# Expert-list selection by 256-element steps over both lists and a tree of additions, in a two-layer transformer kernel on one core

## The reference, cut to what matters

```python
v1, i1 = lax.top_k(s1, PEER_TOPK)              # 16 of 128 keys, first list
v2, i2 = lax.top_k(s2, PEER_TOPK)              # 16 of 128 keys, second list
cand = (v1[..., :, None] + v2[..., None, :]).reshape(T, PEER_HEADS, 256)
cidx = (i1[..., :, None] * PEER_NKEYS + i2[..., None, :]).reshape(T, PEER_HEADS, 256)
sv, pos = lax.top_k(cand, PEER_TOPK)
eidx = jnp.take_along_axis(cidx, pos, axis=-1)
gw = jax.nn.softmax(sv, axis=-1)
...
hact = jax.nn.gelu(act) * gc                   # act = x . u_tab[eidx]
y = hact @ v_tab[eidx]
```

## Time and profile before

| | us |
|---|---|
| median of 3 runs | 2060.24 |
| lowest and highest of the 3 | 2059.74, 2060.33 |
| profiled execution, first to last instruction | 2053.1 |
| PE busy in it | 1996.7 (97%) |
| DVE busy | 1576.0 (77%) |
| ACT busy | 1121.1 (55%) |
| POOL busy | 280.8 (14%) |

### The profile page before, as it was taken

One profiled execution on the slowest core, in us unless ns is written; L12 is line 12 of the kernel. 1 busy time (PEld: TensorE's weight loads), 2 busy tenths in 40 slices (PEclk: granted clock), 3 DMA queues, 4 the chain that ended last, 5 costly groups with the idle time before them and its releaser, 6 DMA issues.

```text
span 2053.1 us, 39743 instructions
## 1 busy us (share of the span) xinstructions
PE 1996.7 (97%) x16490; PEld 1944.6 (95%) x16490; DVE 1576.0 (77%) x2806; ACT 1121.1 (55%) x1743; POOL 280.8 (14%) x265
## 2 busy tenths in 40 slices
PE   7999998999999999999999999999999999999998
PEld 7899988999999999999999999998889999999998
DVE  6888689785999777787777788664668887877764
ACT  5578678545444666654444455474445554445553
POOL 0000000002888544430000000000100000000000
PEclk9999999999999999999999999999999999999999
DMA  5444433657555343446766777433025677655553
GB/s 198 167 156 139 159 127 119 212 200 258 186 187 186 138 143 139 142 147 224 266 237 239 274 265 256 154 135 143 17 69 214 248 244 272 216 184 173 185 179 121
DMA packets 104435, 375.53 MB, mean 183 GB/s; under 512 B 11584, under 2 KB 12096, under 8 KB 103872
## 3 DMA queue, kind: packets, MB, share of 16 engines
q1 hardware_dynamic: 104256, 372.99, 52.1%
HBM read 370.84 MB, written 2.10 MB: 182 GB/s over the span
## 4 chain that ended last, share of the span: by engine, by line
PE 73%; DVE 19%; ACT 3%; issue 2%; DMA 2%; SPq 0%; POOLq 0%; POOL 0%; DVEq 0%; ACTq 0%
PE ps L377 20%; PE ps L378 20%; PE ps L379 20%; DVE wl L1562 3%; PE ps L784 3%; DVE arenap L1939 3%; ACT wh L1110 1%; DMA raw<-in_ada 1%; PE ps L463 1%; DVE arenap L1904 1%; PE ps L464 1%; PE ps L465 1%; DVE arenap L1899 1%; DVE arenap L1902 1%; DVE arena L1674 1%
## 5 line engine op out<-in xcount | busy, mean ns | idle before, releaser
L377 PE MATMUL ps<-xah,wh 128*128 128x256 f32 x2800 | 797.9, 285 | 6.6 <-DVE wl L1562 5.9
L378 PE MATMUL ps<-xal,wh 128*128 128x256 f32 x2800 | 787.4, 281 | 0.0
L379 PE MATMUL ps<-xah,wl 128*128 128x256 f32 x2800 | 787.1, 281 | 0.0
L1110 ACT ACTIVATE wh<-raw 128x1024 fp32r<-128x1024 f32 (+1 forms) x608 | 622.2, 1037 | 292.3 <-PE ps L379 140.7
L1562 DVE TENSOR_TENSOR wl<-raw,wh 128x1024 fp32r<-128x1024 f32 (+2 forms) x539 | 638.3, 1204 | 171.5 <-ACT wh L1110 170.3
L377 PEld LDWEIGHTS ps<-xah,wh 128*128 128x128 f32 x2800 | 528.3, 189 | 20.0 <-issue 9.8
L378 PEld LDWEIGHTS ps<-xal,wh 128*128 128x128 f32 x2800 | 528.5, 189 | 0.5 <-issue 0.2
L379 PEld LDWEIGHTS ps<-xah,wl 128*128 128x128 f32 x2800 | 528.4, 189 | 0.0
L2317 POOL TENSOR_TENSOR wl<-raw,wh 128x1024 fp32r<-128x1024 f32 (+1 forms) x69 | 163.1, 2370 | 1136.3 <-ACT wh L1110 1136.2
L377 PE MATMUL ps<-hh,wh 128*128 128x256 f32 x1024 | 289.5, 283 | 5.8 <-DVE wl L1562 5.8
L378 PE MATMUL ps<-arenar,wh 128*128 128x256 f32 x1024 | 287.7, 281 | 0.0
(11 more groups left out here) (353 smaller groups left out, 2959.6 us busy)
## 6 DMA issues: line engine op xcount, KB each, us to landing
raw<-in_pu SPq DMA_DIRECT2D x128, 512.0 KB, 3.3
raw<-in_pv SPq DMA_DIRECT2D x128, 512.0 KB, 3.7
raw<-in_ada SPq DMA_DIRECT2D x96, 512.0 KB, 4.3
raw<-in_ff_up SPq DMA_DIRECT2D x88, 512.0 KB, 4.3
raw<-in_w_xbc SPq DMA_DIRECT2D x32, 512.0 KB, 3.2
raw<-in_ff_down SPq DMA_DIRECT2D x32, 512.0 KB, 4.0
raw<-in_w_z SPq DMA_DIRECT2D x16, 512.0 KB, 3.2
raw<-in_w_so SPq DMA_DIRECT2D x16, 512.0 KB, 4.5
```

The lines of the kernel that those rows point to most:

```text
L377: mm(o, w0, x0, start=start, stop=False, skip_group_check=skip)
L378: mm(o, w0, x1, start=False, stop=False, skip_group_check=skip)
L379: return mm(o, w1, x0, start=False, stop=stop, skip_group_check=skip)
L1110: put(W.hi(i), W.raw(i), ACT.Copy).then_inc(S["high"], 1)
```

## The change

It makes `eq` 16 rows of 256 elements, and treats both lists in one instruction: for each token half, 16 `scalar_tensor_tensor` of 256 adjacent elements (2 lists x 128), one for each candidate, and then four additions of 8 x 256, 4 x 256, 2 x 256 and 1 x 256 elements, of which the last writes `isel`. The scratch grows from 2,048 to 4,096 elements a partition. A wait on DVE's own semaphore is added ahead of L1945 (now L1950). Lines from L1933 on move by one to five.

```diff
-        eq, lists = view(arp, 80, 128, 16), view(scp, 0, 3, 256)
+        eq, lists = view(arp, 80, 16, 256), view(scp, 0, 3, 256)
...
+                both_pos = arp[:, 124 * 256:126 * 256].rearrange("p (s n) -> p s n", s=2)
                 for tt in range(2):
-                    for s, p in ((0, posh), (1, posl)):
+                    v.wait_ge(own.sem, own.n)
+                    p2 = both_pos[:, :, tt * 128:tt * 128 + 128]
+                    first = if16[:, tt].rearrange("p s h k -> p (s h) k")
+                    for j in range(16):
+                        last = stt(eq[:, j, :].rearrange("p (s n) -> p s n", s=2), p2, float(j),
+                                   first[:, :, j:j + 1].to_broadcast([128, 16, 16]), ALU.is_equal, ALU.mult)
+                    last.then_inc(own.up(), 1)
+                    for n in (8, 4, 2):
                         v.wait_ge(own.sem, own.n)
-                        e4 = eq.rearrange("p (h k) j -> p h k j", k=16)
-                        p3 = p[:, tt * 128:tt * 128 + 128].rearrange("p (h k) -> p h k", k=16)
-                        for j in range(16):
-                            last = stt(e4[:, :, :, j], p3, float(j), if16[:, tt, s, :, j:j + 1].to_broadcast([128, 8, 16]),
-                                       ALU.is_equal, ALU.mult)
-                        last.then_inc(own.up(), 1)
-                        v.wait_ge(own.sem, own.n)
-                        nc.vector.tensor_reduce(isel[:, s, tt * 128:tt * 128 + 128], eq, X, ALU.add).then_inc(own.up(), 1)
-                        yield
+                        tt_(eq[:, 0:n], eq[:, 0:n], eq[:, n:2 * n], ALU.add).then_inc(own.up(), 1)
+                    v.wait_ge(own.sem, own.n)
+                    tt_(isel[:, :, tt * 128:tt * 128 + 128], eq[:, 0, :].rearrange("p (s n) -> p s n", s=2),
+                        eq[:, 1, :].rearrange("p (s n) -> p s n", s=2), ALU.add).then_inc(own.up(), 1)
+                    yield
+                v.wait_ge(own.sem, own.n)
                 tt_(gw3, sv3, sv3[:, :, 0:1].to_broadcast([128, 16, 16]), ALU.subtract).then_inc(S["gw_sub"], 1)
```

## The result

| | before | after |
|---|---|---|
| median, lowest and highest of 15 runs each, us | 2058.49 (2053.87 to 2060.33) | 2062.32 (2059.80 to 2065.78) |
| profiled execution, first to last instruction, us | 2053.1 | 2060.5 |
| ratio after / before | | 1.0019, 95% interval 1.0013 to 1.0026 |

The change costs 0.19%, which is 3.9 us (2.7 to 5.4). The forecast was 2062.9, 2.7 us above a median of 2060.24 of three runs; over 15 runs that median is 2058.49. So the absolute time was met more closely (0.6 us) than the difference (1.2 us too small): the forecast started 1.8 us too high and added 1.2 us too little, and that the two nearly cancel is luck.

The account below looks back on a forecast made before the run. PE was taken to bound the kernel, with DVE's selection costing only through PE's wait for the lists. That wait grows by 2.7 us, clock and other terms zero: 2060.24 becomes 2062.9, forecast's own range 2061.2 to 2064.4, overall 2059.0 to 2065.0.

Parts of the forecast that it names:

- What bounds the kernel: PE is busy through the choice of experts except its 1.88 us wait before the list transposes; at most 3.6 us to gain.
- its second part: Behind PE's wait for the lists, 3.4 us at half clock lose 1.7 us, which a shorter selection could give back.
- The lock: DVE instructions reading two SBUF tiles wait for POOL's instruction and hold POOL for their own data pass, 1.04 ns an element.
- The sum: The whole forecast: +2.7 us, all PE's wait for the lists, making the median 2062.9.
- 2.7 us later: Start of L1950, behind the selection on DVE: 2.7 us later than before, central rows 2.9, most results 1.6 to 3.1.
- The stride costs nothing that could be won back: Writing adjacent elements instead of every sixteenth in DVE's steps gains nothing: bounds 0 and 0.02 us each.
- The clock: Half clock behind PE's wait for the lists: no change taken, bounds -0.65 and +1.05 us.
- 7.1 us above the span: The forecast's starting median of 2060.24 us, from three runs, set against the profiled execution of 2053.1 us.
- The faster one: Rival: POOL's lock passes five steps a round whatever their size, PE's wait goes, -3.6 us, 2056.6; chance 0.12.
- The starved PE: Rival: POOL's lateness passes 4.4 us and PE stands at a unit between 630 and 660, 2065.6; chance 0.10.

Follow-up runs that it names:

- e10: Kernel before, with 8 dummy products on PE in its 1.88 us wait: stretch 181.34 us against 181.43, ratio 0.9988 (0.9980 to 0.9997).
- e3: Kernel before, with the two position tables in a PSUM bank: selection 24.65 us against 63.48, ratio 0.9989 (0.9980 to 0.9998).
- e8: Kernel before, with both lists in steps of 256 at stride 16 and one reduce per token half: selection 64.98 us, ratio 1.0015 to before.
- e11: The whole change with positions in PSUM, plus two more 2,048-element additions in the first token half: stretch 179.72 us, ratio 0.9999 to the kernel before.
- e1: The change with one strided reduce per token half in place of the tree of additions: selection 61.66 us, ratio 1.0002 to the kernel before.
- e5: The whole change with the position tables in a PSUM bank: selection 36.08 us, ratio 0.9981 (0.9972 to 0.9989) to the kernel before.

## Why the prediction was right

- **What bounds the kernel.** Right: PE's only new wait is that for the lists, 4.58 us. The most that a shorter selection can give back was put at 3.6 us; the PSUM runs gave 3.58 in the stretch. The reason for its second part was not quite the one stated: by the stretch of e10, the half clock of the kernel before was covered by the chain behind the subtraction, and e3 gets past both at once, because there exp, roundings and `wl` are early too.
- **The lock.** Right, and shown by e3. The order of the queues by rule gave 66.5 us for the new selection (607.06 to 673.6), against 66.16.
- **The sum.** The term "2.7 us later" measured 2.68. A match to 0.02 us is luck, since the rules as written gave 2.9 and the intervals 1.6 to 3.1. The spacing of free steps was taken as 0.37, and is 0.335. So the first sixteen passed as 3, 1, 3, 1, 3, 1, 3, 1, without the last step that the schedule put into the next gap, and the 2,048-element addition was issued at 631.9. It then waited for POOL until 634.16, and so passed in the very gap that the schedule gave it (632.5, which is 634.4 with the 1.86 us by which this trace is later), ahead of the POOL instruction that it was to get ahead of. The wrong spacing thus changed this by only 0.2 us. POOL's instruction beside it took 3.93 us, not over 4, and POOL came 2.4 us late at most, not 2.9. The second half went in the forecast's order, seven steps and later two more behind POOL's instructions, the rest free. L1950 came at 675.08, which is 673.2 without the 1.86 us; 673.3 was forecast.
- **"The stride costs nothing that could be won back"** was wrong. At 128 elements it costs 0.03 us a step (0.235 against 0.20), at 256 it would have cost 0.125 (0.46 against 0.335). It is also the error in the spacing: 0.37 was made from the 0.235 of the strided steps, and is too long by just their 0.035. And it hid why adjacent writing belongs to this change: without it the wide steps lose 1.5 us (e8).
- **The clock**, taken as no change with bounds of -0.65 and +1.05, was mis-sized: the half clock lasted 6.8 us instead of 3.4, PE worked through 6.0 us of it and lost 3.0 us instead of 1.7, and the stretch grew by 3.90 - 2.70 = 1.2 us more than the wait, a little past the upper bound. This is the difference between 2.7 and 3.9. That it lasts 6.8 us behind the longer wait is read from one trace, and is not shown to be so each time: near 447 us PE waits 1.8 us in all thirteen kernels, with the same code up to there, and the low stretch behind it lasted 3.4 us in ten traces and 6.8 in three.
- **"7.1 us above the span"**: the profiled execution after took 2062.32 us for a span of 2060.5, so 1.8 us lie around it. The other 5 were one execution's distance from the median, and a sign that three runs did not fix the median.
- **The rivals.** The faster one, a count of steps to a round whatever their size, fell: a round passes four wide steps instead of five, and only two once POOL has no gap. The starved PE did not come; e11 shows, with the positions in PSUM, that it is real, and two more additions away.

By parts, from the selections: both lists at once at stride 16 +1.5 us (e8), adjacent writing with the strided reduce -3.3 (e1), the tree in place of that reduce +4.5 (after).

## What to carry to other kernels

An instruction count and an unhindered duration say little of DVE work beside POOL: ask of each instruction how many SBUF tiles it reads, and what POOL does at that time. A reduce reads one tile and passes beside POOL; a tree of additions of the same size, each reading two, waits for POOL once per member wherever POOL is at work, and delays it by nearly its own length. Moving one operand to PSUM removed the wait where no rearrangement of the steps did (63.5 to 24.7 us), and what it is worth is read from PE's wait and the half clock behind it, here 3.6 us of the 38.8. A clock term counts only as far as no other chain ends beside it: by the stretch, of 1.7 us lost to it 0.1 came back, and of 3.0 us 1.3.

## What the runs showed of the hardware that was not expected

- DVE at a stride of 64 bytes: steps of 256 elements start 0.46 us apart, against 0.335 when adjacent; the reduce of 4,096 elements takes 7.7 us where neighbours lie 1,024 bytes apart, and 4.42 where they are adjacent. The Trainium skill (SBUF — State Buffer, Specifications) has lines of 16 bytes in SBUF and a penalty for each access that crosses to a new one. By that rule the trace agrees in both cases; in the forecast I had read the stride as free.
- DVE delays POOL by its own data pass less some 0.13 us: 2.41 us became 2.57, 2.85, 3.39 and (e5) 4.41 beside 256, 512, 1,024 and 2,048 elements.
- Filling PE's wait with dummy products, 1.95 to 9.1 us of them, kept the clock at 1.0 behind it in all four traces, and by the stretch gave back less than half of what the half clock seemed to take.
- The same code with the same wait of PE (1.8 us near 447 us) was followed by 3.4 us at 0.5 in ten traces and by 6.8 us in three.
